# A two-sequence encoder layer on one core: the two sequences run in turn, and the gathers of the sparse route are spread over three stages

## The reference

```python
def encoder_layer(x, ...):
    h = rmsnorm(x, norm1_g)
    proj = h @ w_in                       # 1024 -> 3584 columns
    na_q, na_k, na_v, r_q, r_k, r_v, r_g = jnp.split(proj, cuts, axis=-1)
    na_o = neighbourhood_attention(...)   # 8 heads of 64
    ret_o = bidirectional_retention(...)  # 4 heads of 128, gated
    x = x + jnp.concatenate([na_o, ret_o], axis=-1) @ w_out
    return x + peer(rmsnorm(x, norm2_g), peer_w_q, peer_sub_keys, peer_u, peer_v)

def peer(h, w_q, sub_keys, u, v):         # 128 x 128 = 16384 experts, 8 heads, top 16
    q = (ht @ w_q).reshape(T, PEER_HEADS, 2, PEER_HALF)
    s = jnp.einsum('thpd,hpnd->thpn', q, sub_keys)
    # top 16 of each half, top 16 of their 256 sums: 128 experts and gates a token
    a = jax.nn.gelu(jnp.einsum('td,tkd->tk', xt, ue))     # ue = u[experts]
    return jnp.einsum('tk,tkd->td', g * a, ve)            # ve = v[experts]
```

## Time and profile before

| | |
|---|---|
| median of 3 runs | 2622.14 us (2612.92 to 2632.96) |
| the profiled execution | 2621.9 us, span of its instructions 2620.1 us |
| granted TensorE clock over the span | 0.972 |
| busy share | PE 91%, PEld 82%, DVE 66%, ACT 33%, POOL 52% |
| moved by DMA | 555.10 MB, 212 GB/s over the span |
| chain that ended last | PE 43%, POOL 26%, DVE 11%, DMA 8%, issue 8% |

### The profile page before, as it was taken

How to read it: one execution, slowest core, us unless ns; L and a number is a source line. 1 busy time by engine, 2 the same in 40 slices (tenths; PEclk the granted TensorE clock), 3 DMA queues, 4 the chain that set the end, 5 groups by cost and what they waited for, 6 DMA issues and landing times.

```text
span 2620.1 us, 33731 instructions
## 1 busy us (share of the span) xinstructions
PE 2394.0 (91%) x12633; PEld 2158.4 (82%) x12633; DVE 1719.4 (66%) x3313; ACT 871.7 (33%) x1356; POOL 1356.0 (52%) x954
## 2 busy tenths in 40 slices
PE   5999998899999999999986877999999899999997
PEld 5977776799999999998976776887888788888886
DVE  4145437331798888555094956877887778777877
ACT  4234322232333333343332322333333333333333
POOL 1001130000266656644585545788778877888773
PEclk9999999989999999999998998999999999999998
DMA  4111102112455555537749598998999999988996
GB/s 143 65 47 46 56 33 81 57 65 89 151 171 171 176 185 180 166 130 219 231 151 356 176 303 286 322 356 312 323 321 325 316 320 325 322 317 302 330 320 232
DMA packets 233602, 555.10 MB, mean 212 GB/s; under 512 B 32064, under 2 KB 123200, under 8 KB 231776
## 3 DMA queue, kind: packets, MB, share of 16 engines
q1 hardware_dynamic: 164592, 345.04, 38.7%
q0 software_dynamic: 68848, 207.91, 22.7%
HBM read 483.90 MB, written 68.94 MB: 211 GB/s over the span
## 4 chain that ended last, share of the span: by engine, by line
PE 43%; POOL 26%; DVE 11%; DMA 8%; issue 8%; ACT 3%; SPq 1%; DVEq 0%; ACTq 0%; POOLq 0%
PE ps L714 25%; POOL a_got L466 12%; POOL picked L461 12%; PE ps L757 10%; DMA raw<-in_experts 4%; DVE hot_a L1341 4%; DMA picked<-in_experts,vidx 3%; POOL u_lo L472 2%; DVE hot_b L1337 2%; PE ps L793 2%; DVE acc_odd L1398 1%; PE ps L814 1%; ACT sp_hi L634 1%; DVE u_lo L1433 1%; PE ps L803 1%
## 5 line engine op out<-in xcount | busy, mean ns | idle before, releaser
L714 PE MATMUL ps<-ht_hi,sp_hi 128*128 128x384 f32 x2048 | 710.3, 347 | 48.6 <-DVE u_lo L1433 25.1
L714 PE MATMUL ps<-ht_hi,u_lo 128*128 128x384 f32 x2048 | 693.1, 338 | 0.0
L714 PE MATMUL ps<-ht_lo,sp_hi 128*128 128x384 f32 x2048 | 692.2, 338 | 0.0
L461 POOL DMA_INDIRECT picked<-in_experts,vidx x384 | 475.8, 1239 | 207.8 <-issue 108.1
L472 POOL TENSOR_TENSOR u_lo<-raw,sp_hi 128x1024 fp32r<-128x1024 f32 x130 | 340.6, 2622 | 418.6 <-ACT sp_hi L634 418.6
L466 POOL DMA_INDIRECT a_got<-acts,aidx x384 | 483.7, 1260 | 117.1 <-issue 117.0
L714 PEld LDWEIGHTS ps<-ht_hi,sp_hi 128*128 128x128 f32 x2048 | 389.3, 190 | 75.1 <-POOL u_lo L472 40.3
L714 PEld LDWEIGHTS ps<-ht_lo,sp_hi 128*128 128x128 f32 x2048 | 389.6, 190 | 3.6
L714 PEld LDWEIGHTS ps<-ht_hi,u_lo 128*128 128x128 f32 x2048 | 388.7, 190 | 0.0
L714 PE MATMUL ps<-v_hi,w_hi 128*128 128x512 f32 x768 | 311.3, 405 | 73.7 <-DVE w_lo L1421 57.8
L643 ACT ACTIVATE act_g<-ps 128x384 f32<-128x384 f32 x256 | 125.6, 491 | 609.4 <-PE ps L714 604.4
(11 more groups left out here) (183 smaller groups left out, 3431.4 us busy)
## 6 DMA issues: line engine op xcount, KB each, us to landing
raw<-in_experts SPq DMA_DIRECT2D x256, 512.0 KB, 3.9
v_raw<-in_experts SPq DMA_DIRECT2D x128, 512.0 KB, 5.5
raw<-in_front SPq DMA_DIRECT2D x52, 512.0 KB, 3.2
acts<-act_g SPq DMA_DIRECT2D x128, 192.0 KB, 3.5
gates<-stage SPq DMA_DIRECT2D x24, 1024.0 KB, 9.5
g_in<-gates SPq DMA_DIRECT2D x128, 192.0 KB, 5.4
lead_acts<-act_g SPq DMA_DIRECT2D x36, 192.0 KB, 5.4
act_in<-lead_acts SPq DMA_DIRECT2D x36, 192.0 KB, 5.6
```

What stands on the lines that cost most here:

```text
L461: pool.indirect_dma_start(picked[n % SLOTS][:, :], None, v_rows, bass.IndirectOffsetOnAxis(ap=vidx[:, n // P, n % P:n % P + 1], axis=0)).t ...
L714: last = pe.matmul(out, l, r, start=start and k == 0, stop=stop and k == 2, skip_group_check=True)
```

## The change

**In turn.** The first sequence (2 tiles, 256 columns) runs its whole front, then its 128 U steps; then the second sequence (4 tiles, 512 columns) runs its whole front, then its 128 U steps; then the 128 V rows come by themselves. All 52 chunks of the front are loaded and split twice. The second sequence's first norm and its transposes stand between U steps 64 and about 95. Scores aren't parked any more.

**Where the visits go.** The sparse tiles are still 0, 1, 2. 93 visits of tiles 0 and 1 stand in the second front, the other 163 of them in U steps 184 to 255, and the 128 of tile 2 in the V rows from row 8 on. Slots for gathered rows are five.

**Splits.** POOL makes the lo part of U steps 0 to 63, of the even ones up to 126, and of 128 to 183; DVE makes the others. The mask, the cosine part and the gate's product go from POOL to DVE in both fronts; the decay matrices of retention are computed in each front.

**Gates.** The windows are 4 U steps with 8 groups each, at 184, 200 and 216. All activations of the second sequence go to HBM and are read back for tiles 3 to 5 in the V rows (before, 36 of 128).

The core of the diff:

```diff
-EARLY = 1
-DENSE = range(TPH, NT)
-LEAD = 36
-GATES_AT = {TPH: 100, TPH + 1: 128, TPH + 2: 145}
-SLOTS = 6
-VISITS = TPH * P
+FIRST_TILE, TILES = (0, 2), (2, 4)
+SPARSE = 3
+DENSE = range(SPARSE, NT)
+STEPS = 2 * N_KEYS
+GATES_AT = {SPARSE: 184, SPARSE + 1: 200, SPARSE + 2: 216}
+GATE_ROWS = 4
+SLOTS = 5
+VISITS = SPARSE * P
+NORM_AT = 64
+FRONT_VISITS = 93
...
+            if step < 64 or step < N_KEYS and step % 2 == 0 or N_KEYS <= step < N_KEYS + 56:
+                by_pool[step] = len(by_pool) + 1
+            else:
+                by_dve[step] = len(by_dve) + 1
...
+            for step in range(N_KEYS):
+                if step in by_pool:
+                    u_part(step)
+            pool.wait_ge(S["sparse_ready"], 2)
+            pool.wait_ge(S["a_done"], N_KEYS)
+            pick_v(0)
+            for k in range(2):
+                pool.wait_ge(act_out[k], 8 * N_KEYS)
...
+            for n in range(FRONT_VISITS):
+                fetch(n, 0, 2 * P)
+            for step in range(N_KEYS, STEPS):
+                if step in by_pool:
+                    u_part(step)
+            pool.wait_ge(S["sparse_ready"], 3)
+            for n in range(FRONT_VISITS, 2 * P):
+                fetch(n, 0, 2 * P)
...
+            front(0)
+            key_scores(0)
+            for step in range(N_KEYS):
+                scores(step)
+                for i in range(4):
+                    if step == NORM_AT + 14 + 5 * i:
+                        turn(1, 0, i)
+            front(1)
+            key_scores(1)
...
+            first_free = N_KEYS + 56
+            rest = 2 * P - done
+            for step in range(first_free, STEPS):
                 window = gate_window(step)
+                share = rest * (step + 1 - first_free) // (STEPS - first_free) - (done - FRONT_VISITS)
...
+            for r in range(N_KEYS):
+                weights(r)
+                visits(r >= 8)
+                weights_lo(r)
+                if r + 1 < N_KEYS:
+                    v_part(r + 1)
+                visits(8 <= r and r % 8 == 0 and done < VISITS - 8)
```

More of the change, by code:

```diff
@@ L220, in encoder_program @@
         a_in = [S[f"a_in{i}"] for i in range(4)]
-        STEPS = 2 * N_KEYS
-        FIRST_DIRECT = N_KEYS + LEAD
-        rows, placed = [], {}
-        for q in range(N_KEYS):
-            early = q * LEAD % N_KEYS < LEAD
-            n = sum(1 for row in rows if (row < LEAD) == early)
-            rows.append(n if early else LEAD + n)
-            placed[rows[q]] = q
-        def u_split(step):
-            return (S["u_lo"], step + 1) if step < N_KEYS + 2 else (S["u_lo_dve"], step - N_KEYS - 1)
@@ L236, in gate_window @@
-        def gate_window(step):
-            for t, first in GATES_AT.items():
-                if first <= step < first + 8:
-                    return t, 4 * (step - first)
-            return None
-        lead_visits = [0, 0] + [2 if gate_window(N_KEYS + e) else 1 + (e % 3 == 0) for e in range(2, LEAD)]
-        left = VISITS - sum(lead_visits)
-        row_visits = [3 if row >= LEAD else 1 for row in rows]
-        for q in range(N_KEYS):
-            if rows[q] < LEAD and rows[q] % 3 == 0 and sum(row_visits) < left:
-                row_visits[q] += 1
@@ L378, in _ @@
                 store_part(step)
[L379 removed]
+                if step == STEPS - 24:
+                    sp.wait_ge(S["tk_chosen"], NT)
+                    for r in range(2):
+                        load_v(r)
             for t in DENSE:
@@ L1452, in u_parts @@
                 split = max(split, last + 1)
-            for e in range(LEAD):
-                step = N_KEYS + e
+            norm(0, 0, s["g1"])
+            for c in range(AHEAD):
+                lo(0, c)
+            log_decays()
+            front(0)
+            dve.wait_ge(*counted(0, "lo_ready", C_END))
+            dve.wait_ge(S["pool_const"], 3)
+            best_keys(0)
+            best_pairs(0)
+            ranked(0)
+            best_keys(1)
+            choices(0)
+            best_pairs(1)
@@ new lines, in _ @@
+            lo(1, 2)
+            front(1)
+            assert done == FRONT_VISITS, done
+            dve.wait_ge(*counted(1, "lo_ready", C_END))
+            best_keys(2)
+            best_pairs(2)
+            dve.wait_ge(S["sc_done"], 4 * NT)
+            ranked(2)
+            for t in range(3, 5):
+                best_keys(t)
+                choices(t - 1)
+                best_pairs(t)
+                ranked(t)
+            best_keys(5)
+            turned_choice(3)
+            choices(4)
```

1674 lines of the change are left out of this document (867 added, 807 removed).

## The result

The changed kernel takes 2808.85 us (median of 4 runs, 2804.88 to 2810.25); the kernel before took 2619.9 us beside it (4 runs, 2612.92 to 2632.96). The ratio is 1.0713, 95% interval 1.0668 to 1.0757. The forecast was 2785 us, range 2620 to 2900, so the sign is right and the time 24 us too low. The total is nearer than its parts: by stages the fronts missed by +18 us, the V rows by +19 and U steps 0 to 127 by -15, so some of the closeness is luck. The profiled execution took 2804.88 us, with a span of 2803.1 us.

What follows compares the result with a forecast made beforehand. It took POOL's gathers to bound the kernel before from 1606 on, 990 of 997 us. Fronts 762, U steps 500 + 308 + 605, V rows 582 and 27 between and behind gave 2784; forecast 2785 us, range 2620 to 2900.

Steps and rivals of the forecast that it cites:

- the twelve gate steps: In U steps 184 to 255: DVE's list of 16.7 us sets each, 201 us in all, with POOL waiting for slots.
- The 24 steps between windows: In U steps 184 to 255: transfers of U rows, activations and gate parts at 374 GB/s set them, 176 us.
- the rival of late loads: U rows land late behind gate stores, steps between windows take 11 us and V rows 4.8: 2934 us, chance 0.13.
- The last 36: U steps 220 to 255: POOL's 2.3 visits set 6.7 us a step, 228 us after 13 off for rows gathered earlier.
- Their sign: In U steps 220 to 255 POOL is without waits and DVE waits for gathered rows.
- The ring of the first sequence's steps: U steps 0 to 127: a two-slot ring through POOL's lo part, not PE, sets 7.2 to 7.6 us for two steps.
- at 318 GB/s 4.6 us: V rows: moving 1.48 MB a row sets its time; 120 rows at 4.57 us and eight without visits at 4.2.
- The row of 4.47 us: V rows without a U step in the kernel before, with one or two visits; PE's own matmuls are 4.1 us.
- 4.1 each: Second sequence's attention: 32 units at 4.1 us with half of each 1.23 us visit in idle time, 140 us with pipeline.
- The 25 us for the norm: U steps 0 to 127: the second sequence's norm, with ACT and DVE pieces in the ring, adds 25 us to 475.
- The fast rival: POOL was the bound and spreading its work pays, mainly in U steps 188 to 255: 2589 us, 1.3% faster, chance 0.12.
- The rule on POOL's shared interface: POOL shares SBUF interfaces with VectorE, so a visit would get cheaper wherever DVE does less; how far was left open.

Runs made afterwards that it cites:

- light rows: The changed kernel with activations and gates loaded for V rows 0 and 1 only and used again in all others: 2804.66 us.
- experiment 9: The changed kernel with the next head's mask added behind a head's last unit on DVE, not at its first: 2788.15 us.
- Experiment 7: The changed kernel with the 93 visits of the second front moved to U steps 184 to 255: 2993.69 us.
- 11: The kernel before with two visits in every leading U step from the third on, and fewer in the V rows: 2609.94 us, ratio 0.9926.

## Why the prediction was right, and where it was not

**Right, by its own steps.** U steps 128 to 183 at PE's own time: 308 against 307.4. Steps 184 to 255: 605 against 602.2, with the twelve gate steps at 16.4 to 16.6 us but for the first of each window. The 24 steps between windows took 161 us where 176 stood, with ACT waiting for U rows (here 5.90 us) in the way that the rival of late loads described, only not so far:

```profile
1700.47 1.06 ACT L671 ACTIVATE sp_hi<-raw 128x1024 fp32r<-128x1024 f32 x1 [5.90 <-DMA raw<-in_experts]
```

The last 36 took 232 us for 228, 6.4 a step for 6.7. Their sign holds in half: DVE waits for gathered rows 37 times, 49.5 us in all, and a visit passes every 2.9 us, but POOL also waits 29.5 us for slots, and ACT 44.1 us for U rows at a DMA share of 0.95. So POOL's price was right there and transfers held these steps beside it. Between and behind: 27 against 27.6. The ring of the first sequence's steps was named rightly.

**The V rows, 582 for 600.7: the step "at 318 GB/s 4.6 us" failed.** A row with one visit was near (4.52 for 4.57) by the wrong mechanism: light rows leave it at 4.52, moving the visit out of the ring brings it to 4.27. What was missing in the sum is the 15 rows with two visits, 5.95 us on average, some 20 us, and the first eight rows, 5.1 us each and not 4.2, 7 us. The row of 4.47 us with its visits, by which the forecast checked its size, was probably this ring at work; that wasn't tried. It had priced each engine and each transfer alone and no chain through ACT, DVE and PE. In that chain VectorE's visit has its price, while the engine that gathers for it, POOL, is idle half the time.

**The fronts, 762 for 780.3: the term "4.1 each" failed.** Attention was to be 52 + 140 = 192 and took 56 + 173 = 229. The visits' half of it was right: from the first to the last unit's scores the second attention takes 166.9 us, and 151.9 with no visit, so they cost 15 us where 0.52 x 32 = 17 stood. It is the units themselves, with two and four in a head, that were priced too low. 20 us of the 37 are the band's mask (over both fronts, by experiment 9), since I looked at no order on DVE. The rest is there without any visit, with a granted clock of 0.91 in that stretch (0.87 with visits, and waits of up to 4.7 us on PE); its cause is open. The other terms of the fronts missed by -11 to +5 us, -18 in sum: projections 103 for 111, retention's 87 for 82, 144 to 201.5 and 1049 to 1143 151.5 for 148, norms 29 for 40, queries and scores 160 for 165.

**U steps 0 to 127, 500 for 484.9.** A pair of steps takes 7.07 us and not 7.2 to 7.6: the load is not late here. The 25 us for the norm are near by luck: at 3.54 throughout it would be 453, and of the 32 us above that 11 are in steps 80 to 95, where the norm stands, and 22 in steps 0 to 63, where ACT waits 14.4 us in all for late U rows.

**The first step of the second and third window** took 24.7 and 23.2 us where 16.7 stood, 15 us in sum, and it stayed hidden in the total because the steps between windows were 15 us cheaper. DVE comes late to these windows (its timeline, then the ACT instruction behind the first group):

```profile
1716.90 1.27 DVE L1472 SCALAR_TENSOR_TENSOR acc<-picked,wts,acc 128x1024 f32<-128x1024 f32 x1
1718.10 1.30 DVE L1472 SCALAR_TENSOR_TENSOR acc_odd<-picked,wts,acc_odd 128x1024 f32<-128x1024 f32 x1
1719.44 1.22 DVE L1476 TENSOR_TENSOR acc<-acc,acc_odd 128x1024 f32<-128x1024 f32 x1
1720.58 1.32 DVE L1472 SCALAR_TENSOR_TENSOR acc<-picked,wts,acc 128x1024 f32<-128x1024 f32 x1
1721.82 0.68 DVE L1435 TENSOR_TENSOR hot_b<-iota,idx_t 128x512 f32<-128x512 f32 x1
```

```profile
1725.76 0.60 ACT L745 ACTIVATE stage<-ps 128x512 f32<-128x512 f32 x1 [10.16 <-PE ps L995]
```

The share of visits of the step ahead (here with the join of two sums) stands on DVE ahead of the window's first one-hot, 5 us of it. The forecast counted a gate step's list from its own start. That these 5 us are most of the 8 extra was not tried by an experiment of its own.

**The fast rival** (the visits' engine was the bound, and spreading pays) is half true, and it is well that it had a chance. Experiment 7 shows that the place in the front saves some 185 us against the alternative, and 11 shows that relief of the V rows pays in the kernel before too. What kills it is the 157 us that the change costs with no visit in it, plus visits that are no cheaper in sum (171 for 145 by the spans). In the V rows of before no relief could bring more than the 87 us by which they are shorter with no visit at all. The prediction's mark of "near 1500 us" for the end of the second sequence's first U step contradicted its own sum, which puts it near 1270: it was at 1271. Its added activations, "some 50 MB", are 36 by the pages' issues (75.5 MB for 39.3), and no term hangs on them.

**The rule on POOL's shared interface.** In the second front's attention, DVE busy 113 of 173 us, gathers take 942 and 969 ns; before they took 1215 and 1245 with DVE at 79%:

```profile
L462 POOL DMA_INDIRECT a_got<-acts,aidx x33 | 32.0, 969 | 10.1 <-issue 10.1
L457 POOL DMA_INDIRECT picked<-in_experts,vidx x32 | 30.1, 942 | 103.1 <-DVE acc L1472 86.0 <-DVE acc_odd L1472 17.1
```

But in U steps 184 to 255 and in the V rows DVE's share is the same 0.72, and line 457 takes 1238 ns in the one and 1040 in the other. DVE's share alone doesn't set it, and between the attention and the V rows of before the DMA share differs too (0.43 and 0.90). The Trainium skill's rule (GPSIMD Engine Reference, section Specifications), that POOL meets contention on an SBUF interface shared with VectorE, agrees with the trace in the first of these and doesn't foretell the second.

## What to carry to other kernels

Splitting a kernel by sequences to open idle time for another engine has a price of its own, and a kernel with that work taken out shows it in one run: here 157 us, against 143 to 158 us that all the work to be hidden had cost. Before work is put into an engine's "idle" time, find the ring through the engines and write its links down in order: where a piece stands in the ring decides its price (the same visit made a V row 0.6, 0.25 or 0.0 us longer at three places), and the busy share tells nothing of it. The mean price of such a piece hides the last one's: 0.3 us on average, 1.7 to 2.5 at the margin, and a move of thirteen visits to where POOL had room gave what the large change did not.

## What the runs showed of the hardware that I had not expected

- 27% fewer bytes a row changed a row's time by nothing, at a DMA share of 0.89 before and 0.72 after, and yet with the pair of rows 0.5 us shorter loads began to be late, in 20 rows of some 100.
- The granted clock was 0.54 in both norms (11 and 18 us with PE busy 3 and 7 us), and 0.87 in an attention stretch with PE busy 83% of the time, but 0.98 in the first sequence's U steps, also 83% busy, with rests of 1 us every second step.
